# Gathering the U and V rows of an expert as one 16 KB row, pair by pair, in the expert stage of a diffusion backbone layer

## The reference, cut to what matters

```python
v1, i1 = lax.top_k(s1, 16)
v2, i2 = lax.top_k(s2, 16)
cand_s = (v1[..., :, None] + v2[..., None, :]).reshape(t, 8, 256)
best_s, pos = lax.top_k(cand_s, 16)
idx = ...                                   # i1 * 128 + i2 at those positions, (t, 128)
gate = softmax(best_s)
act = gelu(einsum('td,tkd->tk', hb, peer_u[idx]))
out = einsum('tk,tkd->td', act * gate, peer_v[idx])
```

## Time and profile before

| | |
|---|---|
| median of 3 runs | 3572.72 us (3571.36 to 3579.14) |
| the profiled execution | 3575.05 us, span 3573.3 us |
| mean granted clock of PE | 0.956 of full |
| busy share of the span: PE, DVE, ACT, POOL | 91%, 44%, 14%, 25% |
| read from HBM | 972 MB, of it 537 MB by the gathers |

### The profile page before, as it was taken

The page is one execution under the profiler, slowest core; times in us unless marked ns, Lnnn a source line. Parts: engine busy times, 40 slices in busy tenths (PEclk is TensorE's granted clock), DMA queues, the critical chain, the costliest instruction groups (busy, mean ns, idle before and its releaser), DMA issues. The chain is left out here.

```text
span 3573.3 us, 32297 instructions
## 1 busy us (share of the span) xinstructions
PE 3268.4 (91%) x11084; PEld 1985.1 (56%) x11084; DVE 1587.4 (44%) x2951; ACT 506.9 (14%) x1029; POOL 910.6 (25%) x612
## 2 busy tenths in 40 slices
PE   6999999999999999999999999898977878787876
PEld 2457667575857666788788864443333333333332
DVE  6444444343434444322100014656556567656564
ACT  2312112121212122101000001111111111011110
POOL 0011112020211112000000001455545555555553
PEclk7999999999999999999999999999999898989898
DMA  9754544545363544544544476999999999999997
GB/s 360 271 227 163 195 181 179 199 167 209 136 229 140 215 179 178 189 170 169 205 161 144 147 254 249 379 426 427 427 422 426 419 426 424 422 428 427 423 428 311
DMA packets 154223, 994.34 MB, mean 278 GB/s; under 512 B 17929, under 2 KB 30762, under 8 KB 44842
## 3 DMA queue, kind: packets, MB, share of 16 engines
q0 software_dynamic: 73728, 536.90, 35.7%
q1 hardware_dynamic: 67978, 428.00, 32.6%
q10 hardware_dynamic: 12448, 28.55, 2.1%
HBM read 972.18 MB, written 21.20 MB: 278 GB/s over the span
## 5 line engine op out<-in xcount | busy, mean ns | idle before, releaser
L2075 PE MATMUL ps<-gates,diagonal 128*128 128x512 f32 x2048 | 991.6, 647 | 227.5 <-ACT diagonal L1715 227.5
L1034 PE MATMUL ps<-mT,ring 128*128 128x256 f32 (+1 forms) x4096 | 1171.1, 446 | 3.0 <-PEq L217 3.0
L1034 PEld LDWEIGHTS ps<-mT,ring 128*128 128x128 f32 x4096 | 775.0, 190 | 392.6 <-issue 323.0
L2075 PEld LDWEIGHTS ps<-gates,diagonal 128*128 128x128 f32 x2048 | 419.9, 208 | 796.9 <-issue 634.2
L1899 DVE CUSTOM_DVE_ANT_0 u_rows<-u_rows,yhy 128x2048 f32<-128x2048 f32 x256 | 586.3, 2293 | 485.3 <-DMA u_rows<-in_peer_u_dram,expert_index 474.4
L1650 POOL DMA_INDIRECT gates<-in_peer_v_dram,expert_index x256 | 409.5, 1599 | 511.5 <-PE ps L2075 457.1
L1650 POOL DMA_INDIRECT u_rows<-in_peer_u_dram,expert_index x256 | 284.3, 1111 | 140.7 <-issue 128.2
L675 POOL TENSOR_TENSOR dd<-mask_f,dt_g 128x1024 f32<-128x1024 f32 x16 | 30.4, 1898 | 951.3 <-DVE dt_g L936 950.7
L1335 PE MATMUL ps<-mT,ring 128*128 128x256 f32 x1024 | 227.0, 382 | 6.7 <-PEq L623 6.7
L1463 PE MATMUL ps<-yss,ring 128*128 128x256 f32 x1024 | 223.6, 379 | 0.0
L1335 PEld LDWEIGHTS ps<-mT,ring 128*128 128x128 f32 x1024 | 194.8, 191 | 38.0 <-issue 11.9
(11 more groups left out here) (310 smaller groups left out, 2270.3 us busy)
## 6 DMA issues: line engine op xcount, KB each, us to landing
ring<-in_w_stream_dram SPq DMA_DIRECT2D x160, 1024.0 KB, 4.8
ada_tiles<-in_w_ada_dram SPq DMA_DIRECT2D x64, 1024.0 KB, 6.7
ring<-in_w_mix_dram SPq DMA_DIRECT2D x64, 768.0 KB, 4.2
ring<-in_w_mod_dram SPq DMA_DIRECT2D x32, 1024.0 KB, 11.1
ring<-in_w_out_dram SPq DMA_DIRECT2D x32, 1024.0 KB, 6.2
rows<-cum_rows_scratch SPq DMA_DIRECT2D x16, 1536.0 KB, 13.0
ring<-in_w_q_dram SPq DMA_DIRECT2D x16, 1024.0 KB, 9.0
hf_c<-hf_scratch SPq DMA_DIRECT2D x8, 1024.0 KB, 7.3
```

Of the source, the lines that this page charges most:

```text
L1034: mm = nc.tensor.matmul(ps[:, k % 4, 0:n], m.ring[:, slot, kt * P:(kt + 1) * P], m.mT[:, kt, 0:n], start=(kt == 0), stop=(kt == KT - 1))
L2075: return nc.tensor.matmul(ps[:, 4 * t + b, :], dia[:, (h % 2) * S + n, :], v_slot[n][:, b * CH:(b + 1) * CH], start=first and n == 0, stop ...
```

## The change

U and V are put side by side in one table `peer` of 16,384 rows of 16 KB, outside the program. The same eight rows of buffer become four **pair** slots of 16 KB: pairs 0 and 1 in `m.u_rows`, pairs 2 and 3 in the space of `m.gates`. One gather brings the U and the V row of an expert, so a batch has four gathers of 2 MB. The slot is free when PE has used the V half (`pair_free`); `dot_v` now counts the dot products. DVE, ACT and PE handle each pair by itself: dot product, gelu of one column, one coefficient, one diagonal (one set of four), four pieces on PE. The index copy comes after the first dot product. The selection work is cut in parts, one after each pair: `rank_halves` in three, `rank_pairs` in four, `weigh` after pair 2. The last batch is gathered by halves (four U rows, then four V rows, from the same table seen as 8 KB rows), with its own indices `idx2`.

```diff
-        u_slot = [m.u_rows[:, n, :] for n in range(S)]
-        v_slot = [v_rows[:, n, :] for n in range(S)]
+        half_rows = [m.u_rows[:, n, :] for n in range(S)] + [v_rows[:, n, :] for n in range(S)]
+        u_half, v_half = half_rows[0::2], half_rows[1::2]
+        pair = [rows[:, n:n + 2, :].rearrange("p a b -> p (a b)") for rows in (m.u_rows, v_rows) for n in (0, 2)]
...
-        dia = sb("diagonal", [P, 2 * S, P])
+        dia = sb("diagonal", [P, S, P])
...
-                with pool.Fori(0, UNITS) as u:
-                    for h in range(NB):
-                        pool.wait_ge(idx_v, NB * u + (h + 1))
-                        for slots, table, into, free in ((u_slot, d.peer_u, u_in, u_free), (v_slot, d.peer_v, v_in, v_free)):
-                            for n in range(S):
-                                pool.wait_ge(free, TOPK * u + (S * h + n + 1))
...
+                def batch(u, h):
+                    pool.wait_ge(idx_v, NB * u + (h + 1))
+                    for n in range(S):
+                        pool.wait_ge(pair_free, TOPK * u + (S * h + n + 1))
+                        gather(n, pair[n], d.peer, idx[:, h % 2, :], pair_in)
...
+                pool.wait_ge(idx_v, NB * UNITS + 1)
+                halves = d.peer.rearrange("e (a n) -> (e a) n", a=2)
+                for n in range(S):
+                    pool.wait_ge(pair_free, TOPK * UNITS - S + n + 1)
+                    gather(n, u_half[n], halves, idx2[:, 0, :], pair_in)
+                for n in range(S):
+                    gather(n, v_half[n], halves, idx2[:, 1, :], last_in)
...
-                    act.wait_ge(u_free, TOPK * u + (S * h + 2 * S))
-                    nc.scalar.activation(gel[:], dot[:], ACT.Gelu_apprx_tanh).then_inc(gel_a, 1)
-                    act.wait_ge(co_v, NB * u + (h + 1))
                     for n in range(S):
-
-                        if not first:
-                            act.wait_ge(v_free, TOPK * u + (S * h + n + 1 - S))
-                        nc.scalar.activation(dia[:, (h % 2) * S + n, :], m.ident[:], ACT.Copy, scale=co[:, n:n + 1]).then_inc(dia_a, 1)
+                        act.wait_ge(dot_v, TOPK * u + (S * h + n + 1))
+                        nc.scalar.activation(gel[:, n:n + 1], dot[:, n:n + 1], ACT.Gelu_apprx_tanh).then_inc(gel_a, 1)
+                        act.wait_ge(co_v, TOPK * u + (S * h + n + 1))
+                        act.wait_ge(pair_free, TOPK * u + (S * h + n + 1))
+                        nc.scalar.activation(dia[:, n, :], m.ident[:], ACT.Copy, scale=co[:, n:n + 1]).then_inc(dia_a, 1)
...
                     for n in range(S):
-                        v.wait_ge(u_in[n], 16 * step + 16)
-                        nc.vector.tensor_tensor_reduce(out=u_slot[n], in0=u_slot[n], in1=h2[:, t, :], scale=1.0, scalar=0.0,
-                                                       op0=ALU.mult, op1=ALU.add, accum_out=dot[:, n:n + 1]).then_inc(u_free, 1)
...
-                    v.wait_ge(gel_a, step + 1)
-                    v.wait_ge(dia_a, S * step)
-                    nc.vector.tensor_tensor(co[:], gel[:], gate[:, span(TOPK * u + S * h, S)], ALU.mult).then_inc(co_v, 1)
...
+                        v.wait_ge(pair_in[n], 16 * step + 16)
+                        nc.vector.tensor_tensor_reduce(out=u_half[n], in0=u_half[n], in1=h2[:, t, :], scale=1.0, scalar=0.0,
+                                                       op0=ALU.mult, op1=ALU.add, accum_out=dot[:, n:n + 1]).then_inc(dot_v, 1)
...
+                        v.wait_ge(gel_a, S * step + (n + 1))
...
+                        nc.vector.tensor_tensor(co[:, n:n + 1], gel[:, n:n + 1], gate[:, span(TOPK * u + (S * h + n), 1)], ALU.mult).then_inc(co_v, 1)
+                        if last:
+                            continue
+                        if h == 0 and n < 3:
+                            rank_halves(u + 1, n)
+                        elif h == 1:
+                            rank_pairs(u + 1, n)
+                        elif h == 2 and n == 2:
+                            weigh(u + 1)
...
-        "peer_u": p["peer_u"], "peer_v": p["peer_v"],
+        "peer": np.concatenate([p["peer_u"], p["peer_v"]], 1),
```

More of the change, by code:

```diff
@@ L1700, in exps, with batch @@
                     nc.scalar.activation(ex[:], arg[:], ACT.Exp).then_inc(ex_a, 1)
-                def batch(u, h, first=False, last=False):
+                def batch(u, h, last=False):
                     if h == 2 and not last:
@@ L1827, in after @@
                     cs.inc(nc.vector.memset(idle[:, k:k + 1], 0.0))
[L1829 to L1842, removed]
-                    for a in range(2):
-                        n = cs.inc(nc.vector.max_index(bidx[:, a, 8:16], best[:, a, 8:16], scan2[:, a, :]))
-                    v.wait_ge(sel, n)
@@ new lines, in rank_halves @@
+                def rank_halves(unit, part):
+                    if part == 0:
+                        n = cs.inc(nc.vector.tensor_copy(scan, scores[:, span(2 * unit, 2), :]))
+                        after(n, 0)
+                        for a in range(2):
+                            cs.inc(nc.vector.max(best[:, a, 0:8], scan[:, a, :]))
+                    elif part == 1:
+                        after(cs.now(), 1)
+                        for a in range(2):
+                            cs.inc(nc.vector.max_index(bidx[:, a, 0:8], best[:, a, 0:8], scan[:, a, :]))
+                            cs.inc(nc.vector.match_replace(scan2[:, a, :], best[:, a, 0:8], scan[:, a, :], -3.0e38))
+                    else:
+                        after(cs.now(), 2)
+                        for a in range(2):
+                            n = cs.inc(nc.vector.max(best[:, a, 8:16], scan2[:, a, :]))
+                        after(n, 3)
+                        for a in range(2):
+                            cs.inc(nc.vector.max_index(bidx[:, a, 8:16], best[:, a, 8:16], scan2[:, a, :]))
@@ new lines, in batch @@
+                        nc.vector.tensor_tensor_reduce(out=u_half[n], in0=u_half[n], in1=h2[:, t, :], scale=1.0, scalar=0.0,
+                                                       op0=ALU.mult, op1=ALU.add, accum_out=dot[:, n:n + 1]).then_inc(dot_v, 1)
+                        if n == 0 and last and h == NB - 2:
+                            for a in range(2):
+                                nc.vector.tensor_scalar(idx2[:, a, :], eidx[:, UNITS * TOPK - S:], 2.0, float(a), ALU.mult, ALU.add).then_inc(idx_v, 1)
+                        elif n == 0 and not (last and h == NB - 1):
+                            nc.vector.tensor_copy(idx[:, 1 - h % 2, :], eidx[:, span(TOPK * u + (S * h + S), S)]).then_inc(idx_v, 1)
@@ new lines, in gate_ffn @@
+                def gate_ffn():
+                    v.wait_ge(rows2_in, 48)
+                    v.wait_ge(pair_free, S + TOPK * PH)
+                    for n in range(4):
+                        cols = slice(n * CH, (n + 1) * CH)
+                        nc.vector.tensor_tensor(gated[:, cols], gt2[:, cols], ps[:, n, :], ALU.mult).then_inc(fin_v, 1)
+                    v.wait_ge(fin_v, 4)
+                    n = c.inc(nc.vector.scalar_tensor_tensor(m.h[:, 0, :], m.h[:, 0, :], ALPHA, gated, ALU.mult, ALU.add))
+                    v.wait_ge(st, n)
```

143 lines of the change are left out of this document (69 added, 74 removed).

## The result

The changed kernel takes **3599.03 us** (median, 3598.31 to 3600.45) where the kernel before takes 3572.1 us on the same chip: ratio 1.0071, 95% interval 1.0055 to 1.0087, 27 us slower. The profiled execution took 3600.45 us, its span is 3598.7 us.

The account below looks back on a forecast made before the run. The prediction took the gather stage to be bound by its DMA bytes. Its terms, -8 + 15 + 3 - 1 - 4 = +5 us on the median of 3572.7, gave 3578 us, range 3561 to 3598.

Parts of the forecast that it names:

- What bounds the kernel: In the gather stage, time lasts as long as the bytes do: 536.9 MB at 427.5 GB/s, 1256 us; all engines wait for data.
- Long rows, -8 us: In the gathers, 16 KB rows and one completion instead of two halve the packet boundaries: -8 us.
- Margin of 4.5 us: In a slot's loop, 10.1 us against 14.6 us of queue for three pairs leaves 4.5 us (3.1 to 4.9).
- The holes, +15 us: Between batches, blocks on DVE and projection pieces on PE outlast the margin and empty the DMA queue: +15 us (0 to 30).
- The start was called neutral: At the first row product, after projections both kernels have, the first four pairs are the same 8 MB: no cost.
- Unit 8: Behind `gate_ffn` and statistics on DVE, 7.15 + 2.2 - 4.5 gives a 4.9 us hole; `finish` falls into it: 0.
- Last batch, +3 - 1: At the end, U gathers wait for whole pairs, +3 us; PE can start with V0 at its landing, 1 us back.
- Waits of before that go, -4 us: In the gather stage, half of 9 us lost at 425 instead of 428 GB/s is waits the new order replaces: -4 us.
- No holes: Between batches, a margin of 7 us or more makes the blocks cost nothing: 3563 us, chance 0.17.
- faster bytes: In the gathers, the whole 1.2% of packet boundaries goes and no holes appear: 3556 us, chance 0.05.
- The loop that is too long in every unit: From batch 1, loop and lag pass 14.6 us, each of 15 units loses 1 us or more: 3595 us, chance 0.14.
- The rival of slow rows: In the gathers, long rows go as two packets or as slowly as 12 KB rows: 3586 to 3609 us, chance 0.14.

Follow-up runs that it names:

- experiment 1: Changed kernel with each pair slot filled by two gathers of 8 KB rows (U half, V half) instead of one: 3606.67 us.
- Experiments 2: Changed kernel without the query work of later heads, every unit using unit 0's scores: 3553.68 us; the kernel before, cut the same way: 3549.07 us.
- 4: Changed kernel with PE's projection pieces for later queries cut in quarters, one after each pair: 3592.06 us.
- 5: Changed kernel with DVE's normalisation of later queries cut in four parts, one per pair, and selection one batch later in these units: 3586.36 us.
- Experiment 9: On experiment 6: pairs 252 to 254 gathered as whole rows, four early projection pieces moved between the first four pairs: 3564.9 us.
- experiment 8: Changed kernel with ACT writing each diagonal seven times more before the one that counts: 3745.13 us.
- Experiment 7: Changed kernel with U and V halves gathered in the old order, the U half free after its dot product, pairwise processing kept: 3576.24 us.
- experiment 6: Changed kernel with PE's projection pieces, DVE's query normalisation and unit 8's gating, statistics and norm all cut into parts behind single pairs: 3573.7 us.

## Why the prediction was nearly right in kind and wrong in size

- **What bounds the kernel**: right. In the ten runs the time follows the bytes, the rate of a full queue and the holes in it. "All engines wait for data" does not hold everywhere, though: from 2500 to 2525 us of the changed kernel PE is busy for all 25 us at full clock, and the DMA share is 0.86.
- **Long rows, -8 us**: right. At the undisturbed rates (86.23 MB in 200 us against 42.76 in 100) 536.9 MB take 10.3 us less, experiment 1 gives 7.6, and the packets fell to 37,440 as forecast. The 12 KB rows at 420 GB/s were no guide. That no fixed cost of a gather was there to save was right as well: 252 gathers fewer, and 8 to 10 us. By the Trainium skill ("DMA: Bandwidth & Descriptors", Anatomy of one DMA) it would have been some 500 us, an estimate. This trace does not bear that out for a full queue: at a share of 1.01 no such time stands between gathers.
- **Margin of 4.5 us**: right in kind, somewhat too large. The loop has 3.23 (forecast 3.66), 4.51 (3.73 with POOL's wake-up) and 3.0 us (2.7; 7.90 less 4.87), which leaves 3.8, or 3.6 by the waiting time in the queue. (The forecast's lower end of 3.1 does not follow from its own terms: 3.3 us for issue and transfer give 3.9, POOL's slow instruction 3.3, both together 2.7.) Steady state free, right: 431 GB/s and PE's clock at 1.00 in units 9 to 14.
- **The holes, +15 us: this step failed**, by 14 us or more. The holes forecast are there, behind batch 1 of units 0, 4 and 8, but they are not alone. Units 0 to 4 and the half of unit 8 gained 29.4 us of lag in the table (3.0 + 6.1 + 9.9 + 3.3 + 7.1); the long rows can have hidden up to 3 us more there (88 of 256 pairs of 8 to 10 us), so the holes cost 29 to 33 us. Three reasons:
  1. *Each hole was counted alone, from a full margin.* In units 0 to 3 PE has 14 us of row products, a projection piece of 3.5 us and the queries' small products in the 19.5 us of a batch (263 of 300 us busy in the window), so after a hole it catches up slowly (from 2500 to 2525 us it has no idle time at all), and I read that the next block then meets a loop without margin. Units 1 to 3 were given 2.9 us of holes and cost 9.9; 4.5 of it lie in pairs 40 to 47, behind unit 2's block, which had been given 0.7. Experiments 2, 4 and 5 show that the query work is the cause: 22 us for all of it (the start's 3 us among them), 7.0 from cutting PE's pieces alone, 12.7 from cutting DVE's. How much margin each block met was not measured.
  2. *The start was called neutral.* The first four pairs are the same 8 MB, but before, the U slots came free at their dot products and the next U rows were queued (by 2272.5 us) while PE still projected. Now POOL stands still for 27.56 us and the queue runs dry: 3 us in pairs 0 to 7, the share 0.93 against 1.01. Experiment 9 takes it away.
  3. *Unit 8*, 6.8 instead of 4.9 us. The block's delay (8.4 us with the clock) was even below the forecast's 9.35 (7.15 + 2.2), but the margin was nearer 1.6 than 4.5, for the most part because POOL's gather meets one of the dot products that DVE makes back to back behind a block and takes 2.37 us. The prediction names this term, 1.2 us beside a dot product, and leaves it out of the sum. That `finish` costs nothing in that hole was right.
- **Last batch, +3 - 1**: right, 2.6 us in the traces. The rows land 3.1 us later, since V rows wait behind U gathers that wait for whole pairs, as said. Behind the last landing 0.5 us come back, half of what was forecast: PE does start when the first V rows land, but after 9.79 us of waiting it runs at half clock (granted 0.52 from 3567.8 to 3574 us).

```profile
3567.79 10.07 PE L2097 MATMUL ps<-u_rows,diagonal 128*128 128x512 f32 x16 [9.79 <-DMA u_rows<-in_peer_dram,expert_half_index]
```

- **Waits of before that go, -4 us**: mostly not seen. Before had a share of 1.00 or 1.01 even where its rate was lowest (413 GB/s in the earlier trace rows, 420 from 3000 to 3100 us), so its queue was full and had few waits to give back. In pairs 144 to 247 the lag falls by 5.8 us, where the long rows explain 3 to 4; the rest, some 2 us, is all that may belong to this term.
- **The rivals.** No holes and faster bytes fell with the windows. The loop that is too long in every unit is not what the changed kernel does (units 9 to 14 are full); experiment 8 shows holes in units 9 to 14 once 3.3 us are added to the loop. The rival of slow rows had the right time, 3586 to 3609 us, for a reason that did not occur.

**Where the expected gain went**: the 8 to 10 us of the long rows are there. Some 35 us were lost against them because one release point, PE's row product, replaced two. Experiment 7 puts the second release and the old order back, and the loss against the kernel before is gone; experiment 6 keeps the single one and takes away most of what stands before it, and it is gone too.

**Open**: whether the order of the gathers (U rows first) or the early release of the U half does more in experiment 7; they were changed together. How fast the margin comes back behind a hole is open too.

## What to carry to other kernels

When a change merges two buffers, ask for each when it was free before: the merged one is free at the later of the two, and the queue's depth is what the difference costs. Work out the margin of that loop, and then hold it against *all* blocks in the in-order streams of *all* engines in the loop, one after the other and not one by one, because an engine that is nearly full gives the margin back slowly, if at all (so I read this case). Long rows are then worth their 0.7% of this stage's rate, if the blocks are cut to the size of the slack between two pairs: 3564.9 us here, 0.3% less than before.

## What the runs showed of the chip that I had not expected

- A loop over a ring of buffers can, it seems, have two steady states. With 0.6 us of margin left by the sum, gaps of 2.8 to 4.1 us on PE were followed by bursts that began at half clock (10.20 us for 16 records in the cycle shown, against 7.03), and gap and burst came again batch after batch: 379 instead of 431 GB/s. In the kernel without the added writes, gaps of 1.14 us leave the clock at 1.00.
- POOL's gather instruction takes 0.94 us in the undisturbed stretch and 2.25, 2.37 and 2.52 us in the rows above where DVE is busy with a long instruction; in this kernel the late gathers meet one. Of its 260 gathers in the changed kernel, the 207 that had no DVE instruction of over 2 us beside their first 0.9 us took at most 1.2 us; of the other 53, 31 took more than 1.5.
- POOL starts its next instruction 4.51 us after the start of a row product of 3.70 us: 0.8 us from PE's end to POOL, where 0.3 us had been assumed.
